# Weight sums by accumulating DMAs, and two matmuls of three joined, in the seven-product pairs of a two-block transformer kernel

## The reference, cut to what matters

```
h  = modulated rmsnorm(x)                 # 512 tokens x 2048
g  = h @ w_gate ;  u = h @ w_up           # 2048 x 5632 each: 44 tiles of 128 hidden columns
f  = silu(g) * u
x += gate * rmsnorm(f @ w_down)
```

## Time and profile before

| what | value |
|---|---|
| time, median of 3 runs | 3155.69 us (3154.74 to 3157.31) |
| profiled execution: time, span of its trace | 3154.46 us, 3152.8 us |
| TensorE, VectorE, ScalarE, GpSimd busy | 98%, 70%, 36%, 24% |
| TensorE in the chain that ended last | 95% of the span |
| seven-product pairs in the trace | 1806.7 to 2655.1 us |
| VectorE busy in that stretch, GpSimd busy | about 84%, 57% |
| weight loads and saves there | 117 GB/s, 34% of the DMA engines' time |

### The profile page before, as it was taken

How to read it: one execution, slowest core, us unless ns; L and a number is a source line. 1 busy time by engine, 2 the same in 40 slices (tenths; PEclk the granted TensorE clock), 3 DMA queues, 4 the chain that set the end, 5 groups by cost and what they waited for, 6 DMA issues and landing times.

```text
span 3152.8 us, 46304 instructions
## 1 busy us (share of the span) xinstructions
PE 3093.9 (98%) x17768; PEld 2696.1 (86%) x17768; DVE 2220.2 (70%) x2659; ACT 1135.1 (36%) x1522; POOL 759.6 (24%) x589
## 2 busy tenths in 40 slices
PE   8999999999999999999999799999999999999998
PEld 7888877888878888888788699999999998888887
DVE  6666566868885444555778988888888886666665
ACT  5323343213233333444532444444444443222223
POOL 0111100111100000000011465555555553122113
PEclk9999999999999999999999899999999999999999
DMA  4444455775752222222366333333333334455544
GB/s 186 144 135 126 125 189 193 295 271 214 263 213 91 81 84 76 81 80 79 154 261 239 124 121 120 111 113 114 112 119 120 120 120 160 164 189 193 189 163 171
DMA packets 106170, 480.97 MB, mean 153 GB/s; under 512 B 20736, under 2 KB 21008, under 8 KB 68816
## 3 DMA queue, kind: packets, MB, share of 16 engines
q1 hardware_dynamic: 63920, 321.15, 28.8%
q0 software_dynamic: 38256, 130.36, 11.5%
q10 hardware_dynamic: 3888, 28.03, 2.3%
HBM read 435.17 MB, written 37.76 MB: 150 GB/s over the span
## 4 chain that ended last, share of the span: by engine, by line
PE 95%; DVE 3%; DVEq 1%; ACT 0%; DMA 0%; issue 0%; ACTq 0%
PE PS L1309 15%; PE PS L1311 15%; PE PS L1310 15%; PE PS L1730 9%; PE PS L1733 9%; PE PS L1732 9%; PE PS L1760 5%; PE PS L1762 5%; PE PS L1761 5%; PE PS L1578 1%; PE PS L1605 1%; PE PS L1362 1%; PE PS L1363 1%; PE PS L1364 1%; PE PS L1593 1%; PE PS L1475 0%
## 5 line engine op out<-in xcount | busy, mean ns | idle before, releaser
L1309 PE MATMUL PS<-XHL,WH 128*128 128x512 f32 x1968 | 775.2, 394 | 5.1 <-DVE WL L1772 2.1
L1311 PE MATMUL PS<-XHL,WL 128*128 128x512 f32 x1968 | 766.1, 389 | 0.0
L1310 PE MATMUL PS<-XHL,WH 128*128 128x512 f32 x1968 | 766.0, 389 | 0.0
L2597 DVE TENSOR_TENSOR QL<-RAW,QH 128x1024 fp32r<-128x1024 f32 x210 | 437.5, 2098 | 38.2 <-ACT QH L1157 37.9
L821 ACT ACTIVATE WH<-RAW 128x2048 fp32r<-128x2048 f32 x138 | 263.8, 1912 | 522.5 <-PE PS L1311 513.6
L1309 PEld LDWEIGHTS PS<-XHL,WH 128*128 128x128 f32 x1968 | 369.4, 188 | 93.1 <-issue 10.6
L1311 PEld LDWEIGHTS PS<-XHL,WL 128*128 128x128 f32 x1968 | 369.4, 188 | 77.6
L1310 PEld LDWEIGHTS PS<-XHL,WH 128*128 128x128 f32 x1968 | 369.6, 188 | 77.1 <-issue 2.2
L1772 DVE TENSOR_TENSOR WL<-RAW,WH 128x2048 fp32r<-128x2048 f32 x138 | 316.5, 2294 | 79.0 <-ACT WH L821 78.9
L1157 ACT ACTIVATE QH<-RAW 128x1024 fp32r<-128x1024 f32 x210 | 222.1, 1058 | 257.8 <-PE PS L1733 256.0
L1730 PE MATMUL PS<-XHL,QH 128*128 128x256 f32 x1008 | 286.2, 284 | 7.0 <-DVE FO L2592 7.0
(11 more groups left out here) (375 smaller groups left out, 5896.3 us busy)
## 6 DMA issues: line engine op xcount, KB each, us to landing
RAW<-w_units_dram SPq DMA_DIRECT2D x268, 1024.0 KB, 4.8
ADA<-w_ada_dram POOLq DMA_DIRECT2D x192, 512.0 KB, 5.5
FR<-f_dram SPq DMA_DIRECT2D x11, 1024.0 KB, 5.5
spill_dram<-SIG POOLq DMA_DIRECT2D x24, 256.0 KB, 2.3
f_dram<-TMP SPq DMA_DIRECT2D x22, 256.0 KB, 5.3
f_dram<-FO SPq DMA_DIRECT2D x22, 256.0 KB, 5.3
BB<-x_t_dram ACTq DMA_DIRECT2D x1, 4096.0 KB, 13.4
x_dram<-RES ACTq DMA_DIRECT2D x1, 4096.0 KB, 14.8
```

The source lines that it names most:

```text
L1309: pe.matmul(PS[:, bank, :], wh, rh[:, x, :], start=k == 0, stop=False)
L1310: pe.matmul(PS[:, bank, :], wh, rl[:, x, :], start=False, stop=False)
L1311: ins = pe.matmul(PS[:, bank, :], wl, rh[:, x, :], start=False, stop=k == n - 1)
L2597: v.tensor_tensor(QL[:, slot, :], weight(s2, j), f32(QH[:, slot, :]), ALU.subtract).then_inc(q_lo, 1)
```

## The change

Two things change in the 42 pairs.

First, the two matmuls with the high weight become one: high and low data stand beside each other as 2 x 256 moving columns, and the result fills a whole bank of 512 columns. The low weight's matmul still has 256 columns and adds to the left half. So a bank holds two halves whose sum is the product. All copies and combinations of banks now work on 512 columns, and VectorE adds the two halves at the end, once for gate (`ST_GATE`) and once for up (`ST_UP`), before Silu and multiplication. Silu stays at 512 columns.

Second, the four weight additions of a pair are accumulating DMAs, issued by GpSimd (`accum_op=ALU.add`, SBUF to SBUF, 512 KB each). There are two tiles SUMS, one for each of the two buffers of weights; SP loads g0 into it a second time from memory (another 512 KB for each pair), and the DMAs add u0 and then u1 to it, u1 to u0, and the sum to g1. GpSimd's loop over pairs is written out.

```diff
-                        y = PS[:, bank, 0:HALF_S]
-                        pe.matmul(y, wh, x[:, 0, :], start=k == 0 and j not in (3, 5, 6), stop=False,
+                        pe.matmul(in_halves(PS[:, bank, :]), wh, x, start=k == 0 and j not in (3, 5, 6), stop=False,
                                   skip_group_check=True)
-                        pe.matmul(y, wh, x[:, 1, :], start=False, stop=False, skip_group_check=True)
-                        ins = pe.matmul(y, wl, x[:, 0, :], start=False, stop=k == FULL_K - 1, skip_group_check=True)
+                        ins = pe.matmul(PS[:, bank, 0:HALF_S], wl, x[:, 0, :], start=False, stop=k == FULL_K - 1,
+                                        skip_group_check=True)
...
-    SUM3 = at("SUM3", T0 + 9696, [P, FULL_K * P])
-    SUM2 = at("SUM2", T0 + 3040, [P, FULL_K * P])
+    SUMS = [at("SUM0", T0 + 9696, [P, FULL_K * P]), at("SUM1", T0 + 3040, [P, FULL_K * P])]
...
     def staged(i):
-        return ST[:, 0, i, HALF_S:S]
+        return ST[:, :, i, HALF_S:S]
...
@@ SP
+            sp.dma_start(SUMS[0][:, :], w_units[U_FFN + 2 * PLAIN, :, 0:FULL_K * P]).then_inc(pair_loaded[0], 16)
...
+            sp.wait_ge(f_made, PLAIN)
+            sp.dma_start(SUMS[1][:, :], w_units[U_FFN + 2 * PLAIN + 2, :, 0:FULL_K * P]).then_inc(pair_loaded[1], 16)
...
+                    sp.dma_start(SUMS[e % 2][:, :], w_units[bass.ds(8 * i + (U_FFN + 2 * PLAIN + 2 * e + 4), 1), :, 0:FULL_K * P]
+                                 .rearrange("a p n -> p (a n)")).then_inc(pair_loaded[e % 2], 16)
@@ GpSimd
-                gp.tensor_tensor(SUM3[:, :], g[:, 0:h], u[:, 0:h], ALU.add).then_inc(sum_ready, 1)
-                gp.drain()
-                gp.tensor_tensor(u[:, 0:h], u[:, 0:h], u[:, h:2 * h], ALU.add).then_inc(sum_ready, 1)
...
+            def sum_3(r, loaded):
+                g, u = RAWS[r][:, 0, :], RAWS[r][:, 1, :]
+                gp.wait_ge(pair_loaded[r], loaded)
+                gp.dma_start(SUMS[r][:, :], u[:, 0:h], accum_op=ALU.add).then_inc(first_sums, 16)
+            def sum_1(s, r):
+                u = RAWS[r][:, 1, :]
+                gp.wait_ge(first_sums, 32 * s + 16)
+                gp.dma_start(u[:, 0:h], u[:, h:2 * h], accum_op=ALU.add).then_inc(first_sums, 16)
+            def sum_2(s, r):
+                gp.wait_ge(q_lo, PRODUCTS * s + (Q0 + 2))
+                gp.dma_start(SUMS[r][:, :], RAWS[r][:, 1, h:2 * h], accum_op=ALU.add).then_inc(later_sums, 16)
+            def sum_4(s, r):
+                gp.wait_ge(q_lo, PRODUCTS * s + (Q0 + 4))
+                gp.wait_ge(later_sums, 32 * s + 16)
+                gp.dma_start(RAWS[r][:, 0, h:2 * h], SUMS[r][:, :], accum_op=ALU.add).then_inc(later_sums, 16)
+            def weight_sums(s, e, loaded):
+                r, n = e % 2, (e + 1) % 2
+                sum_2(s, r)
+                gp.wait_ge(first_sums, 32 * s + 32)
+                sum_3(n, loaded)
+                sum_4(s, r)
+                sum_1(s + 1, n)
@@ ScalarE
             def half_copied(i, bank, done):
                 act.wait_ge(q_done, done)
-                act.activation(staged(i), PS[:, bank, 0:HALF_S], ACT.Copy).then_inc(copied, 1)
+                act.activation(staged(i), in_halves(PS[:, bank, :]), ACT.Copy).then_inc(copied, 1)
...
             def gated(s):
-                act.drain()
-                act.wait_ge(taken, 4 * s + (TAKEN0 + 4))
-                act.activation(staged_pair(1, ST_G), staged_pair(0, ST_G), ACT.Silu).then_inc(silu_done, 1)
+                act.wait_ge(gate_summed, s + 2)
+                act.activation(staged(ST_GATE), staged(ST_GATE), ACT.Silu).then_inc(silu_done, 1)
@@ VectorE, end of a pair
                 v.tensor_tensor(staged(ST_G + 1), bank(2), staged(ST_V), ALU.subtract).then_inc(taken, 1)
+                v.drain()
+                v.wait_ge(copied, 3 * s + (COPIED0 + 3))
+                v.tensor_tensor(staged(ST_GATE), *both(ST_G), ALU.add).then_inc(gate_summed, 1)
+                v.tensor_tensor(staged(ST_UP), *both(ST_U), ALU.add).then_inc(up_summed, 1)
```

More of the change, by code:

```diff
@@ L139 @@
 FULL_K = DT // 2
-NEED_SUM = {1: 1, 2: 2, 4: 3, 6: 4}
 NEED_T = {1: 2, 2: 1, 4: 4, 5: 3}
@@ L280, in build @@
     DS = SM1[:, 40:48]
-    ST_P1, ST_V, ST_G, ST_U = 0, 1, 2, 4
+    ST_P1, ST_V, ST_G, ST_U, ST_GATE, ST_UP = 0, 1, 2, 4, 6, 7
     FHS = [FH, at("FH1", X0 + 32 * K, [P, FF_CHUNK, S], FP32R)]
@@ L288, in staged @@
     def staged(i):
-        return ST[:, 0, i, HALF_S:S]
-    def staged_pair(a, i):
-        return ST[:, a, i:i + 2, HALF_S:S]
+        return ST[:, :, i, HALF_S:S]
     def in_halves(ap):
@@ L299, in weight @@
         g, u, h = RAWS[s2][:, 0, :], RAWS[s2][:, 1, :], FULL_K * P
-        return [g[:, 0:h], SUM3[:, :], u[:, 0:h], g[:, h:2 * h], SUM2[:, :], u[:, h:2 * h], g[:, h:2 * h]][j]
+        return [g[:, 0:h], SUMS[s2][:, :], u[:, 0:h], g[:, h:2 * h], SUMS[s2][:, :], u[:, h:2 * h], g[:, h:2 * h]][j]
     def f32(ap):
@@ L358, in build @@
         pair_loaded = [sem("pair_loaded0"), sem("pair_loaded1")]
[L359 to L362, removed]
+        first_sums, later_sums, q_hi, q_lo, q_done, copied, taken = (
+            sem(n) for n in ("first_sums", "later_sums", "q_hi", "q_lo", "q_done", "copied", "taken"))
+        t_sum, t_hi, t_lo, gate_summed, up_summed, silu_done, f_made = (
+            sem(n) for n in ("t_sum", "t_hi", "t_lo", "gate_summed", "up_summed", "silu_done", "f_made"))
         turn_loaded = [sem("turn_loaded0"), sem("turn_loaded1")]
@@ L579, in _ @@
                 gp.tensor_tensor(BB[:, t, :], BB[:, t, :], RES[:, t, :], ALU.add).then_inc(x3_ready, 1)
[L581 to L585, removed]
-                gp.tensor_tensor(SUM3[:, :], g[:, 0:h], u[:, 0:h], ALU.add).then_inc(sum_ready, 1)
-                gp.drain()
-                gp.tensor_tensor(u[:, 0:h], u[:, 0:h], u[:, h:2 * h], ALU.add).then_inc(sum_ready, 1)
[L589 to L593, removed]
-                gp.wait_ge(q_lo, PRODUCTS * s + (Q0 + 4))
-                gp.tensor_tensor(g[:, h:2 * h], g[:, h:2 * h], SUM2[:, :], ALU.add).then_inc(sum_ready, 1)
@@ L597, in _ @@
[L597 to L602, removed]
+            h = FULL_K * P
+            def sum_3(r, loaded):
+                g, u = RAWS[r][:, 0, :], RAWS[r][:, 1, :]
+                gp.wait_ge(pair_loaded[r], loaded)
+                gp.dma_start(SUMS[r][:, :], u[:, 0:h], accum_op=ALU.add).then_inc(first_sums, 16)
@@ L604, in ada_load @@
+            def weight_sums(s, e, loaded):
[5 more added lines that the diff above has]
+                sum_1(s + 1, n)
+            sum_3(0, 48)
+            sum_1(0, 0)
+            for s in range(FAST - 1):
+                weight_sums(s, s % 2, 48 * ((s + 1) // 2 + 1))
+            sum_2(LOOPED + 1, 1)
+            sum_4(LOOPED + 1, 1)
             def ada_load(n):
@@ L1154, in hi_part @@
                 act.wait_ge(q_done, done)
-                if j in NEED_SUM:
-                    act.wait_ge(sum_ready, 4 * s + NEED_SUM[j])
+                if j in (1, 2):
+                    act.wait_ge(first_sums, 32 * s + 16 * j)
+                if j in (4, 6):
+                    act.wait_ge(later_sums, 32 * s + 16 * (j // 2 - 1))
                 act.activation(QH[:, slot, :], weight(s2, j), ACT.Copy).then_inc(q_hi, 1)
@@ L1184, in fast_pair @@
                     if j == 2:
-                        act.wait_ge(f_made, s + PLAIN)
+                        act.wait_ge(up_summed, s + 1)
                         half_copied(ST_U + 1, 7 - 4 * s2, q + 2)
                     if j == 4:
+                        act.wait_ge(gate_summed, s + 1)
                         half_copied(ST_G, 4 - 4 * s2, q + 4)
@@ L1213, in _ @@
             plain_silu(1)
-            act.wait_ge(pair_loaded[0], 32)
+            act.wait_ge(pair_loaded[0], 48)
             for j in range(2):
@@ L1229, in _ @@
                 for e in range(4):
-                    fast_pair(4 * i + e, e, 64 * i + 32 * ((e + 1) // 2 + 1))
-            fast_pair(LOOPED, 0, 32 * (LOOPED // 2 + 1))
+                    fast_pair(4 * i + e, e, 96 * i + 48 * ((e + 1) // 2 + 1))
+            fast_pair(LOOPED, 0, 48 * (LOOPED // 2 + 1))
             fast_pair(LOOPED + 1, 1, 0, False)
@@ L1832, in _ @@
             v.drain().then_inc(copied, COPIED0)
+            v.drain().then_inc(gate_summed, 1)
+            v.drain().then_inc(up_summed, 1)
             def by_step(ap):
@@ L2597, in lo_part, with both @@
                 v.tensor_tensor(QL[:, slot, :], weight(s2, j), f32(QH[:, slot, :]), ALU.subtract).then_inc(q_lo, 1)
+            def both(i):
+                return (ST[:, a, i:i + 2, HALF_S:S] for a in range(2))
             def fast_pair(s, e, saved, more=True):
@@ L2604, in bank @@
                 def bank(i):
-                    return PS[:, b0 + i, 0:HALF_S]
+                    return in_halves(PS[:, b0 + i, :])
                 for j in range(2, PRODUCTS):
@@ L2632, in fast_pair @@
                 v.wait_ge(f_saved[e % 2], saved)
```

(2 more changed lines are left out.)

## The result

| | before | changed |
|---|---|---|
| median of 13 runs | 3155.81 us (3153.99 to 3157.45) | 3136.22 us (3134.47 to 3151.29) |
| ratio | | 0.9950, 95% interval 0.9942 to 0.9959 |
| profiled execution: time, span | 3154.46 us, 3152.8 us | 3136.03 us, 3134.3 us |

The change makes the kernel 0.5% faster, 19.6 us, where 32.7 us were forecast. The time lies in the stated range and outside the 3118 to 3130 us given to the likeliest case. The runs of before lie within 3.5 us. Those of the changed kernel don't: nine lie at 3134 to 3137 us and four at 3147 to 3151 us.

A forecast was written before the change was run, and what follows sets the result against it. The prediction took TensorE, busy without a gap, as the bound: 3154.46 - 31.0 (matmuls) - 1.5 (start) + 1.1 (end) = 3123.1 us, 1.0% faster; the range to hold 8 in 10 was 3118 to 3175 us.

The forecast's parts named there:

- the likeliest case: Whole kernel: all goes as forecast, 3123 us, with its own range of 3118 to 3130 us; chance 68%.
- What bounds the stage: The 42 pairs: TensorE is busy without a gap, 20.16 us a pair, and stays the bound at 19.41 us.
- TensorE's part: Matmuls of the pairs: a step falls from 0.3600 to 0.3467 us over 2352 steps; 31.0 of 31.4 us taken as saved.
- GpSimd and VectorE: In a pair: without GpSimd's additions low parts take 1.22 us, and VectorE needs 14.0 us of 19.4, 17.0 before.
- The accumulating DMA, a = 2.4 us: Weight sums: each takes 2.4 us of the DMA engines, two reads at 442 GB/s; TensorE waits from a = 2.75.
- the planned 93%: DMA engines in a pair: loads and saves 8.4 us plus sums 9.6 us, 18.0 of 19.41 us.
- They fit on average but not in phase: Rival in the pairs: sums and loads wait for each other, 4 to 25 us lost, 3130 to 3149 us; chance 8%.
- the waits of the sums: Sums in the pairs: landing up to 11 us after issue does no harm, 4 to 7 us expected; TensorE doesn't wait.
- Start: Ahead of the first pair: a low part beside GpSimd falls from 3.37 to 1.22 us; 1.5 us taken as saved.
- End: From the last product to the down projection: the chain grows by longer operations and a sum of halves, 1.1 us more.
- The rule of 2.5 ns a matmul: Skill's price for the joined matmuls, not used in the sum: 2.5 ns saved a step, 5.9 us in all.

The follow-up runs named there:

- e2: Changed kernel, but in products 1, 2, 4 and 5 the 512-column matmul names its operand as one piece of 512; median 3137.62 us.
- e4: Changed kernel, but the low weight's matmul has 512 columns too, so all matmuls of the stage have one length; 3371.81 us in one execution.
- e8: The changed kernel as it is, one execution with a profile; 3124.36 us, no waits of TensorE in the stage, 0.3467 us a step.
- e5: Kernel before with only the joined matmul, its 512-column copies and the sums of halves, weight sums still on GpSimd; 3219.04 us, ratio 1.0200.
- e15: The changed kernel as it is, one execution with a profile; 3151.44 us, with 15.3 us of waits of TensorE in the stage.
- e7: The changed kernel as it is, one execution with a profile; 3140.40 us, with 6.0 us of waits of TensorE in the stage.
- e12: Changed kernel with the first sum made early by VectorE and, in each product, eight 512-column matmuls then eight of 256; median 3129.54 us, ratio 0.9919.

## Why the prediction was right or wrong

- **What bounds the stage, and that TensorE stays the bound**: right for the undisturbed executions.
- **TensorE's part, "I take nearly all of it, 31.0 us"**: this is the term that failed. The rows had streams of one length only, and the text named that gap. But its lower bound was filled with the wrong question, whether two pieces start like two matmuls. They don't (e2, e4). What costs is the mixture of lengths: 0 or 6.7 ns a step, 15.7 us in most executions, so that 31.4 - 15.7 = 15.7 us were saved where 31.0 stood. The saved 13.3 ns itself is real, as e8 and e4 show. The reason given, that the 13.3 ns goes with the instruction, thus holds; that the two prices add up in one mixed stream doesn't, in most executions.
- **GpSimd and VectorE**: right. Low parts at 1.22 us, the multiplication at 0.69; VectorE 108.35 / 8 = 13.5 us a pair against 14.0 forecast. That the two parts need each other was right, but 19.8 us for the joining alone was 21.7 (e5), where the new sums of halves, priced at 0.69 us each, took 2.3 and 2.8 us beside GpSimd.
- **The accumulating DMA, a = 2.4 us**: too low, 2.76. That is 1.05 MB of reads in 2.76 us, 380 GB/s, where I had taken 442. It fitted all the same, since the loads took 7.9 us and not 8.4: the planned 93% were 98% in e8. In bytes written it is 0.52 MB in 2.76 us, 190 GB/s, less than half of the 442 of the best slice of copies. The Trainium skill (Collectives: The Full Stack, The bandwidth ceiling) says that the second source read of an adding DMA halves its rate. This trace agrees in kind; the 2.1 us estimated from that page was further off than my 2.4.
- **"They fit on average but not in phase", 8%**: undervalued. By their times 8 of 19 executions of the changed kernel have it (3140 to 3151 us); the four of them with a profile show its waits. The part on the waits of the sums looked at each sum's own slack of 11 us from issue to landing, and the medians of the sums' landings stayed under it (8.5 us at most in e15). It named what stands behind a waiting issue in GpSimd's queue, and held that each is "wanted several products later". That is the step that failed here: the first sum of the next pair may wait up to 8.2 us for its load (e15), and the fourth of this pair is issued only then.
- **Start**: 4.2 us saved, not 1.5. Besides the low part, VectorE's preparation of TA fell from 5.38 to 3.25 us without GpSimd beside it; the trace had that row and the sum left it out. The two rows, before and changed:

```profile
1791.57 5.38 DVE L2652 SCALAR_TENSOR_TENSOR TA<-RES,SM,TA 128x256 fp32r<-128x256 f32 x8
1791.66 3.25 DVE L2680 SCALAR_TENSOR_TENSOR TA<-RES,SM,TA 128x256 fp32r<-128x256 f32 x8
```

- **End**: right, 8.6 us of wait for 7.5.
- **The rule of 2.5 ns a matmul**: the Trainium skill (TensorE: Matmul & The Clock Gate, Back-to-back issue gap) gives an isolated warm gap of N / 2.4 + 2.5 ns. An estimate by it is a saving of 5.9 us and a time of 3148 us. No run shows its 2.5 ns: e4's 0.2267 us a matmul is 13.3 ns over the 0.2133 us of its 512 columns (512 / 2.4 GHz, at a granted clock of 1.00), and the measurement decides.

Put together for a usual run: 3154.5 - 31.4 + 15.7 - 4.2 + 1.1 = 3135.7 us against 3136.03 profiled. The start's 2.7 us more hid a part of the 15.7.

Open: why the step is 0.3467 us in some executions and 0.3533 in others of the same program. It changed at waits of TensorE in e2 and e7, and held where there were none; what chooses it was not found. Nor is it shown what in TensorE makes the extra of a mixed stream; no run varied the weight loads by themselves. Nor is it shown why the loads land late in some executions.

## What to carry to other kernels

Price a matmul by starts in a stream that has the same mixture of lengths; here two pure streams didn't give the mixed one, and grouping equal lengths or turning every other step round got part of it back. A resource planned at over 90% should be priced as a bound even if the sum fits: look for the queue in which one late transfer holds up another that is already due. When a unit is relieved by moving work to DMAs, move back what now has room: one of four sums on VectorE, early enough, took the spread away.

## What the runs showed of the hardware

- An accumulating DMA within SBUF, 128 x 4 KB, takes 2.76 us of the 16 engines when alone and lands 4.5 us after issue there, and 4.6 to 5.3 us (medians) over the first profile; GpSimd is busy 0.86 us with issuing one and 0.53 us with a plain one of that size.
- A 512-column matmul and a 256-column one in turn take 0.3467 or 0.3533 us for the two, in one program, by execution and, in executions with waits of TensorE, by stretch between them; 0.2267 us each if all have 512 and 0.1200 if all have 256. Eight of 512 and then eight of 256 take 2.793 us (e12), where 8 x 0.3467 is 2.773.
- VectorE's 128x1024 subtraction takes 1.22 us alone and up to 3.4 us beside GpSimd's additions.
